# Second block's input projections as three fp32r products of leading parts and rests

## What is computed

```
h    = rms_norm_2(x, norm_w[0, 0]) * (1.0 + scale) + shift      # (256, 1024)
proj = h @ attn_w_in                                            # (1024, 2320)
gq, gk, gv, gg, glr, sq, sk, sv = split(proj)                   # 256,256,512,512,16,512,128,128
log_a = log_sigmoid(glr @ gla_w_gate + gla_b_gate) / 16         # -> GLA decay
o_gla = gla_chunked(gq, gk, gv, log_a);  o_swa = sliding_window_attention(sq, sk, sv, ...)
y     = concat([rms_norm(o_gla) * silu(gg), o_swa]) @ attn_w_out
```

## Time and profile before

| | |
|---|---|
| time, median of 3 runs | 1192.83 us |
| lowest and highest run | 1187.38 and 1197.19 us |
| span of the profiled execution | 1203.7 us |
| PE busy | 1059.8 us, 88% of the span |
| DVE, ACT, POOL busy | 609.3, 347.2, 159.9 us |
| mean granted TensorE clock | 0.914 |

### The profile page before, as it was taken

The page is one execution under the profiler, slowest core; times in us unless marked ns, Lnnn a source line. Parts: engine busy times, 40 slices in busy tenths (PEclk is TensorE's granted clock), DMA queues, the critical chain, the costliest instruction groups (busy, mean ns, idle before and its releaser), DMA issues.

```text
span 1203.7 us, 17491 instructions
## 1 busy us (share of the span) xinstructions
PE 1059.8 (88%) x7244; PEld 789.8 (66%) x7244; DVE 609.3 (51%) x806; ACT 347.2 (29%) x457; POOL 159.9 (13%) x235
## 2 busy tenths in 40 slices
PE   5999977999868899998659998699999977999995
PEld 1689844977435556554238788588888855888884
DVE  0477486655353224332056774676765477543533
ACT  1230034221201111111024133364643225644520
POOL 6302013001000233320030000011111030000000
PEclk9899877988969999999779986899999977999997
DMA  9967658334599999999999630448766281446510
GB/s 332 366 235 251 238 190 300 116 111 167 205 410 403 402 349 399 355 352 347 360 289 368 251 119 22 157 136 294 268 216 238 88 331 44 167 148 231 197 70 35
DMA packets 114104, 287.56 MB, mean 239 GB/s; under 512 B 16415, under 2 KB 42343, under 8 KB 114035
## 3 DMA queue, kind: packets, MB, share of 16 engines
q1 hardware_dynamic: 95538, 247.01, 55.3%
q10 hardware_dynamic: 6544, 25.18, 5.4%
q0 software_dynamic: 11952, 14.38, 3.9%
HBM read 335.79 MB, written 2.62 MB: 281 GB/s over the span
## 4 chain that ended last, share of the span: by engine, by line
PE 71%; DMA 9%; DVE 9%; SPq 4%; ACT 2%; issue 2%; POOL 1%; DVEq 0%; ACTq 0%; POOLq 0%
PE ps L583 30%; PE ps L2342 6%; PE ps L2704 5%; PE ps L2683 3%; DMA arena<-in_moe_w_down_dram 3%; PE ps L2731 3%; PE ps L2344 2%; PE ps L2630 2%; SPq L629 2%; PE ps L2519 2%; PE ps L2809 2%; DMA ring<-in_ada_w_dram 2%; SPq L776 2%; PE ps L2746 1%; DMA arena<-in_moe_w_up_dram 1%
## 5 line engine op out<-in xcount | busy, mean ns | idle before, releaser
L588 DVE TENSOR_TENSOR ring_parts<-ring,arena_parts 128x2048 fp32r<-128x2048 f32 x68 | 153.5, 2286 | 46.5 <-ACT arena_parts L1125 41.2
L583 PE MATMUL ps<-arena_parts,macc_parts 128*128 128x512 f32 x512 | 165.9, 396 | 0.0
L583 PE MATMUL ps<-arena_parts,gate_parts 128*128 128x512 f32 x288 | 115.3, 400 | 9.3 <-DVE hT_parts L588 9.3
L583 PE MATMUL ps<-ring_parts,gate_parts 128*128 128x512 f32 x288 | 113.9, 396 | 0.0
L583 PE MATMUL ps<-arena_parts,hT_parts 128*128 128x512 f32 x288 | 113.7, 395 | 0.0
L583 PEld LDWEIGHTS ps<-arena_parts,macc_parts 128*128 128x128 f32 x512 | 96.2, 188 | 19.5
L583 PE MATMUL ps<-ring_parts,macc_parts 128*128 128x512 f32 x256 | 99.8, 390 | 0.0
L1125 ACT CAST arena_parts<-ring 128x2048 fp32r<-128x2048 f32 x32 | 60.4, 1909 | 79.9 <-issue 40.6
L2342 PE MATMUL ps<-hT,ring 128*128 128x256 f32 x288 | 69.0, 404 | 1.4 <-DVE hT L555 1.4
L583 PEld LDWEIGHTS ps<-arena_parts,gate_parts 128*128 128x128 f32 x288 | 55.3, 192 | 21.9 <-DVE hT_parts L588 10.3
L2704 PE MATMUL ps<-ring,hT 128*32 128x256 f32 x1024 | 62.1, 392 | 7.7 <-issue 4.6
(11 more groups left out here) (560 smaller groups left out, 1711.4 us busy)
## 6 DMA issues: line engine op xcount, KB each, us to landing
ring<-in_mlp_w_dram SPq DMA_DIRECT2D x40, 1024.0 KB, 7.9
arena<-in_moe_w_down_dram SPq DMA_DIRECT2D x16, 2048.0 KB, 11.9
ring<-in_ada_w_dram SPq DMA_DIRECT2D x29, 1024.0 KB, 7.9
ring<-in_mlp_w_dram ACTq DMA_DIRECT2D x24, 1024.0 KB, 7.1
ring<-in_moe_w_up_dram SPq DMA_DIRECT2D x10, 2048.0 KB, 17.4
ring<-in_moe_w_gate_dram SPq DMA_DIRECT2D x10, 2048.0 KB, 21.5
arena<-in_ada_w_dram SPq DMA_DIRECT2D x15, 1024.0 KB, 7.1
ring<-in_w_in_dram SPq DMA_DIRECT2D x13, 1024.0 KB, 5.9
```

The costliest lines, as they stand in the source:

```text
L583: ins = nc.tensor.matmul(o, l, r, start=start and i == 0, stop=stop and i == 2, skip_group_check=True)
L588: return eng.tensor_tensor(lo, x, hi.bitcast(F32), ALU.subtract)
```

## The change

All nine projections and glr become three fp32r products. `hT` is split by ACT (into slot 5 of `ring`) and by DVE (in place, `hT_lo`). Each weight piece is split in two halves of 128 x 1024: ACT copies the leading part into slot 6 or 7 (`in_hi`, i even or odd), and POOL subtracts it from the piece in place. So slots 5, 6 and 7 no longer take pieces: pieces 0 to 4 go to slots 0 to 4, the others to slots as projections free them, and `w_out` pieces to slots 3, 4, 2 and 5. sk and sv are now one group of 256 columns with the weights stationary, so sv comes out transposed, and two PE transposes and one more ACT copy turn it back before the fifth SWA score group.

Beside that: the first five pieces are issued as soon as the experts have freed their slots, ahead of step piece 0, and step pieces 1 to 7 are issued ahead of piece 5. POOL's four memsets and `short` (L1044 to L1053) move from behind the norm to the end of the experts. SP loads MLP slots 0, 1, 6, 7 early and 2, 3, 4, 5 late (it was 0, 5, 6, 7 and 1, 2, 3, 4). The diff, cut to its core:

```diff
+        stream2 = [("in", 0, 0, 0), ("in", 1, 1, 0), ("in", 2, 2, 0), ("in", 3, 3, 0), ("in", 4, 4, 0),
+                   ("in", 5, 0, 1), ("in", 6, 1, 2), ("in", 7, 2, 3), ("out", 0, 3, 4), ("out", 1, 4, 5),
+                   ("in", 8, 0, 6), ("out", 2, 2, 8), ("out", 3, 5, 9)]
+        in_slot = [0, 1, 2, 3, 4, 0, 1, 2, 0]
+        out_slot = [3, 4, 2, 5]
+        in_hi = [ring_lo[:, 6 + i, :].rearrange("p (t n) -> p t n", t=8) for i in range(2)]
+        hT_hi = ring_lo[:, 5, :].rearrange("p (k t) -> p k t", k=KT)
...
-            mod1_in(sp, 0)
             sp_block2(sp)
...
+            pieces = {5: range(1, 8), 6: range(8, 12), 7: range(12, 16), 8: range(16, 20), 11: range(20, 24)}
+            for i, (kind, n, slot_, freed) in enumerate(stream2):
+                if i == 5:
+                    mod1_in(sp, 0)
+                for n1 in pieces.get(i, ()):
+                    mod1_in(sp, n1)
+                if freed:
+                    sp.wait_ge(t_bin, freed)
                 elif i % 4 == 0:
-                    sp.wait_ge(t_gu, 2 * NI - 1 + i // 4)
+                    sp.wait_ge(t_gu, 2 * NI - 2 + i // 4)
...
-            first_chunks_in(sp, 0, (0, 5, 6, 7))
+            first_chunks_in(sp, 0, (0, 1, 6, 7))
             sp.wait_ge(t_bout, 4)
-            first_chunks_in(sp, 0, (1, 2, 3, 4))
+            first_chunks_in(sp, 0, (2, 3, 4, 5))
...
+            def in_trail(i):
+                w, w_lo = (x[:, in_slot[i], :].rearrange("p (t n) -> p t n", t=8) for x in (ring, ring_lo))
+                for half in range(2):
+                    ks = slice(4 * half, 4 * half + 4)
+                    pool.wait_ge(a_in, 2 * i + half + 2)
+                    trailing(nc.gpsimd, w_lo[:, ks], w[:, ks], in_hi[i % 2][:, ks]).then_inc(g_in, 1)
+
+            pool.wait_ge(a_in, 1)
+            trailing(nc.gpsimd, glr_lo, w_glr, glr_hi).then_inc(g_in, 1)
+            for i in range(9):
+                in_trail(i)
...
+            def in_lead(i):
+                if i > 1:
+                    act.wait_ge(t_bin, i - 1)
+                act.wait_ge(ring2[in_slot[i]], in_landed[i])
+                w = ring[:, in_slot[i], :].rearrange("p (t n) -> p t n", t=8)
+                for half in range(2):
+                    ks = slice(4 * half, 4 * half + 4)
+                    nc.scalar.copy(in_hi[i % 2][:, ks], w[:, ks]).then_inc(a_in, 1)
+
+            def first_leads(_):
+                act.wait_ge(par2_in, 16 * 7)
+                act.wait_ge(t_gu, 2 * NI)
+                nc.scalar.copy(glr_hi, w_glr).then_inc(a_in, 1)
+                in_lead(0)
+
+            a_norm_out(act, cn, "bn", *mod_of[0], meanwhile=first_leads, hi=hT_hi)
+            in_lead(1)
...
+                if i < 7:
+                    in_lead(i + 2)
...
             v_norm_out(dve, cn, "bn", *mod_of[0])
+            v_hT_lo(dve, "bn", hT_hi, 0)
             final_out(0)
             final_out(1)
...
+                        if j == 0 and k % 4 == 0:
+                            pe.wait_ge(g_in, 2 * i + k // 4 + 2)
+                        first, last = k == 0, k == KT - 1
+                        if i in (0, 1, 6, 7, 8):
+                            ins = mm3(o, w_hi[:, k, cols], w_lo[:, k, cols], hT_hi[:, k, :], hT_lo[:, k, :], first, last)
+                        else:
+                            ins = mm3(o, hT_hi[:, k, cols], hT_lo[:, k, cols], w_hi[:, k, :], w_lo[:, k, :], first, last)
...
             pe.wait_ge(a["bp"], STEP["bp.a"])
+            for tt in range(TT):
+                ins = nc.tensor.transpose(bin_bank(9)[:, P * tt:P * tt + P], sv_t[:, P * tt:P * tt + P], ident[:, :])
+            ins.then_inc(t_bin, 1)
```

More of the change, by code:

```diff
@@ L761, in sp_block2 @@
         def sp_block2(sp):
[L762 to L767, removed]
+            pieces = {5: range(1, 8), 6: range(8, 12), 7: range(12, 16), 8: range(16, 20), 11: range(20, 24)}
[6 more added lines that the diff above has]
+                    sp.wait_ge(t_bin, freed)
                 elif i % 4 == 0:
-                    sp.wait_ge(t_gu, 2 * NI - 1 + i // 4)
-                if i == RING:
+                    sp.wait_ge(t_gu, 2 * NI - 2 + i // 4)
+                if i == 5:
                     sp.wait_ge(t_dn, 2 * NI)
@@ L1033, in _ @@
                     over_down_in(pool, i)
[L1034 to L1040, removed]
             c = Counter(pool, g["bp"])
-            pool.wait_ge(v["bn"], STEP["bn.v"])
-            pool.wait_ge(t["bn"], STEP["bn.t"])
+            pool.wait_ge(t_dn, 2 * NI)
+            pool.wait_ge(t_gu, 2 * NI)
+            pool.wait_ge(v_sel, 4 * NI)
             c.link(nc.gpsimd.memset(gate2[3][:, :], 0.0))
@@ L1488, in copied @@
                 else:
+                    cp.link(nc.scalar.copy(sv_t, bank[:, 256:512]))
                     for kv in range(2):
@@ L1524, in out_hi_copy @@
             def out_hi_copy(q):
-                act.wait_ge(ring2[(9 + q) % RING], 32)
-                c.link(nc.scalar.copy(out_hi[q], ring[:, (9 + q) % RING, :]))
+                act.wait_ge(ring2[out_slot[q]], ring2_n[out_slot[q]])
+                c.link(nc.scalar.copy(out_hi[q], ring[:, out_slot[q], :]))
                 c.at(f"bs.hi{q}")
@@ L1541, in _ @@
             cp.at("bp.a")
+            act.wait_ge(t_bin, 10)
+            cp.link(nc.scalar.copy(svt[:, :, :], bin_bank(9)[:, 0:256].rearrange("p (a n) -> p a n", a=2)))
+            cp.at("bp.v")
             nc.scalar.activation(swm[:, 48:49], ones[:, 0:1], ACT.Exp)
@@ L2366, in _ @@
             c.at("w.if")
-            nc.tensor.matmul(ps[0:SWA_H, 4, 0:384], rel_sb[0:33, :], hots[0:33, :], start=True, stop=True).then_inc(t_bias, 1)
+            c.mark(nc.tensor.matmul(ps[0:SWA_H, 4, 0:384], rel_sb[0:33, :], hots[0:33, :], start=True, stop=True))
+            c.at("w.ebc")
             for n in (9, 10):
@@ L2884, in _ @@
             pe.wait_ge(a["bp"], STEP["bp.a"])
+            for tt in range(TT):
+                ins = nc.tensor.transpose(bin_bank(9)[:, P * tt:P * tt + P], sv_t[:, P * tt:P * tt + P], ident[:, :])
+            ins.then_inc(t_bin, 1)
             for j in range(6):
+                if bs_bank[j] == 7:
+                    pe.wait_ge(a["bp"], STEP["bp.v"])
                 hs = range(4 * j, 4 * j + 4) if j < 2 else range(2 * (j - 2), 2 * (j - 2) + 2)
```

77 lines of the change are left out of this document (37 added, 40 removed), and 2 rows, old and new, of the table STEP.

## The result

| | before | after |
|---|---|---|
| first series, median | 1194.86 us (4 runs) | 1209.48 us (4 runs) |
| its ratio and 95% interval | | 1.0124 [1.0091, 1.0157] |
| second series, median | 1197.62 us (15 runs) | 1208.04 us (10 runs) |
| its ratio and 95% interval | | 1.0086 [1.0054, 1.0119] |
| span of the first profiled execution | 1203.7 us | 1207.5 us |

The changed kernel is slower, by 10.4 us in the longer series and by 14.6 in the shorter one; the two intervals overlap.

The account below looks back on a forecast made before the run. DVE's order, lengthened by alternating with POOL's subtractions, was taken to bound the stretch up to p6, PE from there. 16.1 - 8.1 + 1.8 + 0.4 - 0.5 = +9.7 us on 1192.8 gave 1202.5, range 1177 to 1213.

Parts of the forecast that it names:

- Rival C: Slower: fp32r products with 256 columns are no shorter than with 512, PE bound throughout; 1221 us, chance 0.06.
- Rival B: Slower: POOL's subtraction costs more in fp32r; 1209.5 us at 2.6 us each, some 1215 at 2.87; chance 0.12.
- Step 1: DVE behind the norm output: both halves of `hT_lo` end at 625.7 us, 1.1 of it blocked; glr ends about 627.7.
- Step 2: DVE's two final-norm operations and step pieces 0 to 7: 12.7 us unblocked, 11.4 for six blocked operations, ending at 650.3.
- Step 3: Scan 2.7 us, ACT's exponentials 2.6, kt 1.4, then pads 1.3, ending at 659.7; PE waits 2 us.
- Step 4: DVE's kend and step pieces 8 to 13, 18.4 us, then 2.7: `bg.at` at 678.1; PE waits some 10 us.
- Step 5: Step pieces 14 to 18 6.6 us, state 5.4, piece 7's halves 3.6, L2156 0.7: p6 at 694.4, 16.1 later.
- Step 6: From p6 on PE bounds: 24.8 us for 32.93, so -8.1; 1.8 charged again for a low clock after idling.
- Step 7: Two PE transposes of sv ahead of the scores: 0.4 us more.
- the MLP's start: ACT's cast of slot 1 is done earlier through early loading: gain between nothing and 1.8 us, taken as 0.5.
- Rival A: Faster: POOL and DVE hardly hold each other up, p6 starts at 672; -12.7 us, so 1180.1; chance 0.22.

## Why the prediction was right, and where it was not

The forecast was 1202.5, +9.7 us; measured were +10.4 (second series) and +14.6 (first), and 1209.48 lies in the range. It is 0.5 us above the narrower 1194 to 1209 that the prediction gave to its own mechanism. The likeliest class was within 1%; the second series is there (0.86%), the first is beyond (1.24%). That the two engines shut each other out, and that this is what made the kernel slower, is shown by the kernel with memsets. That the sum came out so close is in part luck: up to the scores it gave +10.2 us (16.1 - 8.1 + 1.8 + 0.4) for 9.1 measured, while single terms were off by 2 to 4 us in either direction. Step by step, with times of after less 1.7, since its F was that much later:

*PE.* PE's timeline of after, in p1:

```profile
638.30 0.28 PE L593 MATMUL ps<-hT_parts,ring_parts 128*128 128x256 f32 x1
638.42 0.40 PE L593 MATMUL ps<-ring_parts 128*128 128x256 f32 x2
638.66 0.28 PE L593 MATMUL ps<-hT_parts,ring_parts 128*128 128x256 f32 x1
```

Three products start in 0.36 us, one every 0.120; a group takes 5.76 us, for 0.114 and 5.5 foreseen. Rival C is out.

*POOL.* 2.3 us alone, and beside DVE a pair in 3.3: right. Rival B, a dearer subtraction, is out.

*Step 1,* `hT_lo` at 625.7: 628.0. Both halves were blocked (6.57 us for the two), not one in part.

*Step 2,* step 7 done at 650.3: 649.1. Fewer operations were blocked than I counted (three steps and one norm operation, for six). The error of step 1 and this one cancel in part. (The terms as given, 625.7 + 12.7 + 11.4, make 649.8.)

*Step 3,* pads at 659.7: 658.9 (PE's L2883 started at 660.63), with PE's wait 2.1 for 2. This hides two errors as well: L2161 took 2.57 us for 0.43, and ACT's table load of 1.28 us, which I had in the chain, fell into ACT's waiting time.

*Step 4,* `bg.at` at 678.1: 679.5, with PE's wait 12.4 for "some 10". Here, as with L2161, a term was left out. I held operations with one operand in SBUF to be free, and L1204 took 2.72 us for 0.75. The rows had shown it: DVE's copy of 16 elements, with one operand, took 2.10. The Trainium skill, "SBUF — State Buffer", section "Who interferes with whom", says it too: a copy or tensor_scalar of DVE in a mode that uses both port pairs shuts GpSimd out or is shut out. L2161 and L1204 agree, and so does the 1.48 beside memsets, which only write.

*Step 5,* p6 at 694.4: 691.9, 13.6 later than before and not 16.1. The state recurrence wasn't blocked at all. Piece 7's subtractions began only at 693.80, as ACT's lead stood behind the sigmoid of p5 in ACT's queue. So the 3.6 us of this term fall away. The path was the one foreseen: steps 14 to 18 (6.1 us for 6.6), the state recurrence (5.4), and then the first gg multiplication, the one for which p6 waits.

```profile
692.78 1.41 DVE L2200 TENSOR_TENSOR arena<-arena,ps 128x512 f32<-128x512 f32 x2
```

```profile
693.57 0.36 PE L593 MATMUL ps<-ring_parts 128*128 128x256 f32 x1 [1.55 <-ACT arena L1522]
```

The first of the two multiplications ends at 693.47, and p6 starts 0.10 us later; in before it was 0.15 (678.14 and 678.29). The row names ACT's sigmoid of p5, but that ended at 692.65, and by the program p6 needs only the one of p4. PE had not much to spare: p5 took 6.96 us, at a granted clock of 0.84 behind the 12.4 us of waiting, for the 5.76 of a group at full clock, and ended at 692.0; in the third profile of after it ended level with DVE. The chain in order of time of after:

```profile
681.32 3.75 PE ps L2901 x12
685.07 6.96 PE ps L593 x48
...
692.77 7.38 DMA macc<-in_ada_w_dram
700.18 1.30 DVE wup L1207
701.57 3.26 DVE wup L1207
704.92 3.27 DVE wup L1207
...
718.15 1.24 DVE macc L2216
719.45 1.92 ACT arena_parts L1566
```

*Step 6,* "from there PE": I gave 35.0 us less 8.1 and plus 1.8 and 0.4, that is 29.1 up to the scores; it was 30.1. It hides two errors. P6 took 5.9 us at full clock, where I had charged 1.8 for a low one. P8 took 7.4 and not 5.5: behind the last sum PE runs at the low clock for a while (the granted clock in p8 was 0.77). It did so in before, too (0.69 from 702 to 707.5), whose timeline shows it:

```profile
702.25 5.39 PE L2809 MATMUL ps<-hT,ring 128*128 128x256 f32 x16
```

Sixteen at full clock take half of 6.91. My 24.8 us had p8 at full clock, and the 32.93 that they were set against had it low. The chain above doesn't run through PE here, but through a path that the prediction had missed and that came out level with PE's (PE waited 2.4 us ahead of the scores, and 2.1 in before). SP held `w_in` piece 8 for the end of p5 (692.03), and the step piece issued behind it, at 692.77, took 7.38 us to land; steps 20 to 23, two of them blocked by piece 8's halves, the output norm and ACT's cast of `w_out` followed.

*Step 7 and the MLP's start:* O to M is 35.5 against 35.3, so the 0.5 is not to be seen. The wait for the transfer of slot 1 is gone, but PE still waits 4.6 us ahead of M for DVE's half (4.3 before).

*Rival A's price* was wrong by more than half. I put the kernel without blocking at -12.7 us; the kernels without subtractions and with memsets measured 0.9958 and 0.9989, that is -5 and -1 us (-6.2 and -5.4 in F to S). P6 started 4.4 us earlier for 6.3 foreseen, and from there to the scores (674.28 to 707.17) it took 32.9 us for 29.1: p8 8.14 and the last sum 4.26 for 5.5 and 3.5. Most of the 3.8 us is again p8's clock, and the last sum is a part of it. With p8's 1.9 us alone the saving on PE from p6 on is 6.2 us for the 8.1 of the forecast.

## What to carry over

Before work is put on an idle GpSimd, see what VectorE does in that time: each subtraction of 2.3 us kept the VectorE operation that it met waiting for about 2.0 us (3.25 for 1.28), more than the 1.22 in which VectorE does the subtraction itself. A replacement that is as long but reads nothing (three memsets) tells this from plain lateness in one run. And of work that is taken off TensorE only that part counts in which TensorE comes last; here, with nothing blocked, that was some 2 of 13 us by the profiles, if the 4 us of the transfers' order are taken off. When a row names the engine that released a wait, compare when that engine was done with when the wait ended: ahead of p6 they were 0.9 us apart, and another engine was the one.

## What was not expected of the hardware

- VectorE's TENSOR_SCALAR on 128 x 512 words took 2.57 us beside GpSimd's subtractions (L2161 of after) and 0.43 without them (the kernels with copies and with memsets); on 128 x 1024 words 2.72 for 0.75.
- A GpSimd copy of 128 x 1024 words to fp32r takes 1.02 us alone (two in 2.03), and a step of VectorE beside it 1.87 to 2.09 for 1.28. Memsets of the same size, 54 of 0.98 us each, left the steps at 1.285, but not TENSOR_SCALAR (1.48 for 0.75) and COPY (1.05 for 0.17 with 8 columns).
- An fp32r product with 256 columns starts every 0.120 us, little more than half of the 0.2275 with 512 columns.
- The same instructions behind the scores took 20.4 or 27.6 us in two executions of one kernel, at a granted clock of 0.91 or 0.60 between 720 and 740 us.
